# Starting the three moving tiles 32 bytes lower: from 64 to 32 bytes past a multiple of 128

## The reference

```
# first layer: 16 softmax heads of 128 with a forget gate, then a gated FFN with a width-3 convolution
h = h + fox_mixer(rms_norm(h, mix_norm), ...) ; h = h + conv_ffn(rms_norm(h, ffn_norm), ...)
# second layer: 4 gated linear attention heads (chunks of 64), 8 dilated heads, then a gated FFN
q, k, v, r, ga, qb, kb, vb = split(rms_norm(x) @ w_in)
mix = concat(gla_mixer(...), dilated_mixer(...)) ; x = x + mix @ w_out
h2 = rms_norm(x) ; x = x + (silu(h2 @ w_gate) * (h2 @ w_up)) @ w_down      # hidden width 5632
```

## The kernel before, in words

| tile | before | after |
|---|---|---|
| raw, w (weights), xres | 0 | 0 |
| xs, hid2, mix (moving) | 64 | 32 |
| folded_t, vec, qk, qk_n, sq_qk, sq_hi, sq_lo, v_tok, probs, probs_t, tap_g, tap_v, silu_g, hid | 64 | 32 |
| ident, mean_d, mean_h, mean_hr, sq_x, sq_sum, ln_x, rstd, up_g | 0 | 96 |
| up_v | 32 | 0 |
| the tiles of the gated linear attention (g_vtok, g_attn, g_kdtok, g_r and others) | 96 | 64 |

## Time and profile before

### The profile page before, as it was taken

One profiled execution on the slowest core, in us unless ns is written; L12 is line 12 of the kernel. 1 busy time (PEld: TensorE's weight loads), 2 busy tenths in 40 slices (PEclk: granted clock), 3 DMA queues, 4 the chain that ended last, 5 costly groups with the idle time before them and its releaser, 6 DMA issues.

```text
span 2249.7 us, 38813 instructions
## 1 busy us (share of the span) xinstructions
PE 2235.9 (99%) x13082; PEld 1962.1 (87%) x13082; DVE 1613.1 (72%) x2397; ACT 1217.1 (54%) x1586; POOL 56.6 (3%) x78
## 2 busy tenths in 40 slices
PE   8999999999999999999999999999999999999999
PEld 6888888888888888888888888888888888888888
DVE  7777777888888888555567677777676666665554
ACT  7777765655555555444465577645444444443333
POOL 1111100000000000000000000000000000000000
PEclk9999999999999999999999999999999999999999
DMA  6555555555555555555546555565555555556664
GB/s 221 190 178 186 186 168 193 190 196 190 192 187 196 188 193 190 196 195 188 193 158 189 165 178 168 169 197 193 190 191 191 190 193 196 190 193 198 204 198 138
DMA packets 118602, 421.99 MB, mean 188 GB/s; under 512 B 13773, under 2 KB 15973, under 8 KB 118544
## 3 DMA queue, kind: packets, MB, share of 16 engines
q1 hardware_dynamic: 113760, 413.19, 55.3%
q0 software_dynamic: 2048, 5.42, 1.0%
q10 hardware_dynamic: 2736, 2.58, 0.3%
HBM read 419.01 MB, written 3.70 MB: 188 GB/s over the span
## 4 chain that ended last, share of the span: by engine, by line
PE 99%; DMA 0%; DVE 0%; ACT 0%; SPq 0%; issue 0%
PE acc L408 59%; PE acc L417 29%; PE acc L405 3%; PE b_val L405 2%; PE acc L414 2%; PE b_val L414 1%; PE b_score L471 0%; PE b_turn L476 0%; DMA xres<-xt 0%; PE b_mean L484 0%; PE b_score L470 0%; PE b_mean L464 0%; PE b_mean L465 0%; PE b_mean L485 0%; PE b_mean L486 0%; PE acc L444 0%
## 5 line engine op out<-in xcount | busy, mean ns | idle before, releaser
L746 ACT ACTIVATE w<-raw 128x1024 fp32r<-128x1024 f32 x783 | 824.9, 1058 | 809.2 <-PE acc L417 771.4
L1059 DVE TENSOR_TENSOR w<-raw,w 128x1024 fp32r<-128x1024 f32 x783 | 958.4, 1227 | 382.4 <-ACT w L746 379.7
L408 PE MATMUL acc<-xs,w 128*128 128x512 f32 x3832 | 992.6, 394 | 1.6 <-DVE xs L1082 1.6
L408 PEld LDWEIGHTS acc<-xs,w 128*128 128x128 f32 x3832 | 676.1, 188 | 109.6 <-DVE w L1059 2.3
L417 PEld LDWEIGHTS acc<-xs,w 128*128 128x128 f32 x3832 | 533.2, 188 | 55.9
L417 PE MATMUL acc<-xs,w 128*128 128x256 f32 x3832 | 543.0, 277 | 0.0
L408 PE MATMUL acc<-hid,w 128*128 128x512 f32 x1408 | 360.0, 392 | 0.0
L1065 DVE TENSOR_REDUCE folded_t<-acc 128x256 f32<-128x512 f32 x324 | 222.7, 687 | 116.8 <-PE acc L417 94.7
L408 PEld LDWEIGHTS acc<-hid,w 128*128 128x128 f32 x1408 | 247.3, 188 | 37.8
L417 PEld LDWEIGHTS acc<-hid,w 128*128 128x128 f32 x1408 | 194.2, 188 | 19.8
L417 PE MATMUL acc<-hid,w 128*128 128x256 f32 x1408 | 197.5, 276 | 0.0
(11 more groups left out here) (205 smaller groups left out, 1261.7 us busy)
## 6 DMA issues: line engine op xcount, KB each, us to landing
raw<-wstream SPq DMA_DIRECT2D x783, 512.0 KB, 3.3
decay_row<-decay_scratch POOLq DMA_DIRECT2D x16, 128.0 KB, 3.7
out<-xres ACTq DMA_DIRECT2D x16, 128.0 KB, 3.0
xres<-xt SPq DMA_DIRECT2D x3, 512.0 KB, 8.8
dist_scratch<-bias_scratch POOLq DMA_DIRECT2D x8, 192.0 KB, 4.8
toeplitz<-dist_scratch POOLq DMA_DIRECT2D x8, 128.0 KB, 4.3
xres<-xt SPq DMA_DIRECT2D x2, 256.0 KB, 4.3
raw<-wstream SPq DMA_DIRECT2D x2, 256.0 KB, 5.5
```

What stands on the lines that cost most here:

```text
L408: pe.matmul(acc[bank_no][:, :], w_hi, x[:, kc, :, :].rearrange("p a s -> p (a s)"), start=opens, stop=False)
L746: act.activation(whi[slot][:, :], raw[slot][:, :], ACT.Copy).then_inc(hi_ready, 1)
L1059: dve.tensor_tensor(wlo[slot][:, :], raw[slot][:, :], whi[slot][:, :], ALU.subtract).then_inc(lo_ready, 1)
```

## The change

One constant. `xs` begins 32 bytes lower (82,080 in place of 82,112), and with it all that is allocated behind it, `hid2` and `mix` among it (133,280 in place of 133,312). No instruction is added, removed or moved on any engine.

```diff
 PHASE = 256
-X_AT = 192
+X_AT = 160
 UW = BLOCKS * P
```

## The result

The changed kernel takes 2296.27 us, the median of four runs (2296.15 to 2297.75), against 2248.79 us for the kernel before on the same chip. The ratio is 1.0211, with a 95% interval of 1.0198 to 1.0224: slower by 47.5 us. The profiled execution took 2296.17 us, with a span of 2294.4 us and a granted clock of 1.000, so the clock is not the cause.

A forecast was written before the change was run, and what follows sets the result against it. TensorE bounds the kernel; 5,752 long matmuls at 3.3 ns more add 19.0 us, other terms 0: 2251.47 + 19.0 = 2270.5 us profiled, 2.55 less for the median, rounded to 2268. Range 2230 to 2298, the forecast's own 2254 to 2279.

The forecast's parts named there:

- TensorE alone sets the time, and VectorE and ScalarE don't see 32 bytes: Whole kernel: the chain is 99% TensorE; shifted tiles on the other two engines add 0.
- The small matmuls, 0: Two-pass matmuls of 256 columns, such as L471: 3 ns between offsets, under 1 us, taken as 0.
- the faster rival: Long matmuls with a moving tile lose their upper levels, minus 3 ns each; 2231 us, chance 0.32.
- The short matmuls, 0: 5,752 short matmuls with a shifted moving tile: no change, bounds minus 12 us and plus 24 us.
- The sign to look for: In the chain, six short matmuls still at 0.68 us, six long ones at 1.39 in place of 1.37.
- The long matmuls, 3.3 ns: 5,752 long matmuls with a moving tile: one step of 32 bytes more, 3.3 ns each, 19.0 us.
- The value projections, 0 within 4 us: 512 pairs where xs is stationary: already at the poor pace, so 0, bounds plus or minus 4 us.
- the count in 300 us: Matmuls in the second FFN's stage view: 1756 for no change, about 1748 forecast, about 1770 faster, under 1726 much slower.
- the much slower rival: FFN stretches lose the good pace of sixes, 6 to 8 ns a pair; 2293 us, chance 0.08.
- No change: All matmuls: stalls depend on time alone and addresses have no part; 2249 us, chance 0.27.

The follow-up runs named there:

- e7: Kernel before, with all tiles the change moved except xs, hid2 and mix given their changed offsets modulo 128; 2250.43 us.
- e10: Kernel before, with hid2 alone 16 bytes off: distance 48 from the weights in the first layer's down projection, 80 in the second's; 2262.14 us.
- e8: Kernel before, with the opening of the stretches (SETTLE) replaced by six long and six short matmuls three times; 2276.01 us.
- e9: Changed kernel, with the opening of the stretches (SETTLE) replaced by six long and six short matmuls three times; 2297.37 us.
- e1: Kernel before, with the weights (and xres) 32 bytes later and the moving tiles left in place; 2297.68 us.
- e2: Kernel before, with both the weights (and xres) and the moving tiles 32 bytes later; 2250.03 us.
- e5: Kernel before, with the moving tiles at 64 modulo 256, so 192 from the weights in place of 64; 2272.0 us.

## Why the prediction was right or wrong

The sign was right, the size was not: 2268 against 2296, a change of 19 us against 47.5. The time lies within the outer range (2230 to 2298), which reached up into a rival, and outside the forecast's own (2254 to 2279). The sign came with a chance of 0.41, and its argument, that 64 is as far from the weights' offset as a tile can be, isn't borne out: 192 is as far modulo 128 and costs 23 us. That it came out right was in good part luck.

**TensorE alone sets the time, and VectorE and ScalarE don't see 32 bytes.** Right. The rows shown moved by 2 ns at most, and e7 gives 2250.43 us for all small tiles.

**The small matmuls, 0.** Right in size (e7). The reading behind it was wrong. I took the 3 ns of the earlier trace rows for an effect of the offset 64 itself. After the change L471 lies at 32 and has a median of 380 ns, L525 lies at 64 and has 377:

```profile
L471 PE MATMUL b_score<-qk_n x48: 379/380/382, 46.3 to 1460.9; 128*128 128x256 f32 x48
```
```profile
L525 PE MATMUL b_mean<-g_vtok,g_attn x8: 377/377/380, 1196.5 to 1308.2; 128*128 128x256 f32 x8
```

The operation made the 3 ns, and not its address. These rows were what spoke most for the faster rival.

**The short matmuls, 0.** This is the step that failed. I reasoned that their spread of 2 ns left them no level to go to, although I had the other level in hand, 117.5 ns in the eights, and used it only as the upper bound. They rose by 4.0 ns on average, 23.1 us in the two traces, which is that upper bound (24 us) within 1 us. The sign to look for had been six short ones still at 0.68 us; they took 0.71. A steady row shows that a state is held, and not that there is no other.

**The long matmuls, 3.3 ns.** Nearly right in size: 3.9 ns, or 22.0 us for the 19.0 predicted. The reason given, one more step of 32 bytes, is not borne out, since steps of 16 bytes cost nearly as much (e10). The levels before (226, 229, 232) are a cycle through the run and don't move up together.

**The value projections, 0 within 4 us.** Right: their long matmuls stayed at 232.8 and 232.9 ns and the short ones rose by 2.8 ns, 1.4 us.

22.0, 23.1 and 1.4 us make 46.5, against 47.5 in the medians.

**A slip in the signs.** For the forecast the count in 300 us was given as 1748, 343.3 ns a pair. With 3.3 ns more the pair is 345.0 ns, and the count 1739. The measured 1710 lies under the 1726 named for the much slower rival.

**The rivals.** The much slower one, 2293 us, was what happened in place and in size: the FFN no longer holds the good pace of sixes. It had the mechanism for some 27 of the 47.5 us; the other 21 are a pace at 32 that is poorer than the poor one at 64 (e8, e9). I gave it 0.08 because the pace looked too steady to be upset. e8 shows that in the FFN it was a choice between two paces, made at the opening of each stretch. `SETTLE`, an opening of five and eight in otherwise even runs, stood in the code, and the earlier trace rows showed the same matmuls at 348 ns. Read together they say that a steady pace was entered and could be lost. No change and faster are refuted by the result itself; all the other distances tried (0, 32, 48, 80, 96, 128, 160, 192, 224) are slower than 64 too.

**What the Trainium skill states.** The Trainium skill (TensorE: Matmul & The Clock Gate, part 2 on what happens when a matmul is issued) has loading the next weights take no read bandwidth from the running matmul. These runs don't agree that the two streams leave each other alone: moving only the weights by 32 bytes (e1) costs 48 us, and moving both (e2) costs nothing. Whether it is read bandwidth that is lost, no run shows. The Trainium skill (SBUF — State Buffer, Specifications) has lines of 16 bytes; a shift by two whole lines still cost 47.5 us.

What stays open is what inside the memory or the engine makes 64 the good distance. The runs show that it is a relation of the two streams, that it is lost within 16 bytes on either side, that its sign counts, and that its period is not 128. They don't show the mechanism.

## What to carry to other kernels

Where TensorE streams back to back in fp32r with a weight load under every matmul, the distance between the start of the moving tile and that of the weights is a tuning parameter worth up to 2.8% here, and any tile allocated between them can change it by accident. Pin both, scan the distance over 256 bytes and not 128, in steps of 16 or less, and check single stages by their pace per pair, since the cost is paid pair by pair. When the same instruction stream has two paces in one trace, cost a change that touches the streams at the other pace for every matmul of the loop, and look for the code that chooses between them.

## What was not expected of the hardware

- Two matmul streams with the same columns, clock and distance can run for 400 us at 342.2 or at 348.9 ns a pair (mean gaps of the FFN, before and e8), depending on the first three pairs of runs in each stretch, 2276.0 against 2248.8 us in all. The stretches over `mix` kept 343.0 ns either way.
- The sign of the distance counts: 229 ns for a long matmul at 64, 232.5 to 232.8 ns at 192, whichever operand is the weights (before and e5). Short matmuls don't follow this rule.
- Distances 0 and 128, and 32 and 160, cost the same within 1 us with different gaps by place; 64 and 192 are 23 us apart.
